# A two-layer sequence model with a third mixer block on one core: each feed-forward part as one program, and matmuls of constants into an unused bank where TensorE waits

## What is computed

```python
# blocks 0 and 1 (i = 0: SSD scan and mLSTM side by side; i = 1: gated linear attention)
h = rmsnorm(x, norm_g[i, 0]);  y = mixer_i(h)            # ends in a product with w_out
x = x + rmsnorm(y, norm_g[i, 1])
h = rmsnorm(x, norm_g[i, 2])
u = dwconv3(h @ ffn_w_up[i]) + conv_b                    # 1024 -> 2 x 2816, 3 taps over tokens
gate, val = split(u)
x = x + rmsnorm((gelu(gate) * val) @ ffn_w_down[i], norm_g[i, 3])
# block 2: causal attention with an index branch, a gated long convolution (31 taps) with a layer norm,
# attention over a memory, three sigmoid gates that merge them, an output projection, 32 routed experts
```

## Time and profile before

| | us |
|---|---|
| median of 3 runs | 2812.07 (2811.98 to 2815.3) |
| profiled execution, its own time | 2814.07 |
| its span | 2812.2 |
| TensorE busy (matmul records) | 2481.3 |
| VectorE, ScalarE, GpSimd busy | 1490.0, 1030.3, 234.3 |
| mean granted TensorE clock | 0.939 |

### The profile page before, as it was taken

The page is one execution under the profiler, slowest core; times in us unless marked ns, Lnnn a source line. Parts: engine busy times, 40 slices in busy tenths (PEclk is TensorE's granted clock), DMA queues, the critical chain, the costliest instruction groups (busy, mean ns, idle before and its releaser), DMA issues. The chain is left out here.

```text
span 2812.2 us, 33931 instructions
## 1 busy us (share of the span) xinstructions
PE 2481.3 (88%) x12483; PEld 2031.4 (72%) x12483; DVE 1490.0 (53%) x2238; ACT 1030.3 (37%) x1718; POOL 234.3 (8%) x264
## 2 busy tenths in 40 slices
PE   5999996688999897998899989799697888599995
PEld 4777785576888785766688877587486677599994
DVE  4766445544555434744555544367897574433333
ACT  3423332334454335423445433433323533133332
POOL 0000001100000000000000000455141000010111
PEclk9999998889999998999999999899897999699997
DMA  4122232122332421112233322223021021699995
GB/s 140 68 83 90 90 105 75 48 88 60 95 100 82 155 80 61 62 59 75 75 97 97 119 105 75 77 89 111 30 74 47 24 90 46 231 373 368 373 377 208
DMA packets 212860, 330.59 MB, mean 118 GB/s; under 512 B 13861, under 2 KB 109997, under 8 KB 212749
## 3 DMA queue, kind: packets, MB, share of 16 engines
q1 hardware_dynamic: 208013, 312.33, 32.4%
q0 software_dynamic: 4736, 16.78, 2.0%
HBM read 299.99 MB, written 29.10 MB: 117 GB/s over the span
## 5 line engine op out<-in xcount | busy, mean ns | idle before, releaser
L366 PE MATMUL ps<-ffn_h_hi,ffn_w_hi 128*128 128x512 f32 x704 | 275.6, 391 | 10.5 <-DVE ffn_h_lo L361 10.5
L367 PE MATMUL ps<-ffn_h_lo,ffn_w_hi 128*128 128x512 f32 x704 | 275.3, 391 | 0.0
L368 PE MATMUL ps<-ffn_h_hi,ffn_w_lo 128*128 128x512 f32 x704 | 275.0, 391 | 0.0
L366 PE MATMUL ps<-wo_hi,lhs_hi 128*128 128x512 f32 x608 | 242.4, 399 | 34.0 <-DVE lhs_lo L361 34.0
L3912 PEld LDWEIGHTS ps<-expert_x,ring 128*128 128x128 f32 x2048 | 235.8, 193 | 8.1 <-DVE expert_x L3995 3.4
L367 PE MATMUL ps<-wo_lo,lhs_hi 128*128 128x512 f32 x608 | 240.8, 396 | 0.0
L368 PE MATMUL ps<-wo_hi,lhs_lo 128*128 128x512 f32 x608 | 240.7, 396 | 0.0
L3912 PE MATMUL ps<-expert_x,ring 128*128 128x96 f32 x2048 | 235.6, 276 | 3.8 <-DVE expert_x L3995 3.0
L361 POOL TENSOR_TENSOR w_lo<-ring,w_hi 128x512 fp32r<-128x512 f32 (+1 forms) x112 | 160.5, 1434 | 750.9 <-ACT w_hi L518 750.2
L361 DVE TENSOR_TENSOR wo_lo<-ring,wo_hi 128x1024 fp32r<-128x1024 f32 x76 | 93.0, 1223 | 185.5 <-ACT wo_hi L653 185.5
L2245 DVE SCALAR_TENSOR_TENSOR y_tmp<-ps,pcol,y_tmp 128x511 f32<-128x511 f32 x88 | 61.9, 745 | 219.8 <-ACT y_tmp L2217 219.8
(11 more groups left out here) (625 smaller groups left out, 5220.9 us busy)
## 6 DMA issues: line engine op xcount, KB each, us to landing
ring<-in_w_up SPq DMA_DIRECT2D x32, 2048.0 KB, 11.1
ring<-in_ffn_w_up SPq DMA_DIRECT2D x88, 512.0 KB, 4.9
moe_down<-in_w_down SPq DMA_DIRECT2D x32, 1024.0 KB
ring<-in_ab_w_in SPq DMA_DIRECT2D x13, 2048.0 KB, 7.9
ring<-in_w_in SPq DMA_DIRECT2D x11, 2048.0 KB, 7.7
ring<-in_ffn_w_down SPq DMA_DIRECT2D x10, 2048.0 KB, 7.7
ring<-in_c_w_in SPq DMA_DIRECT2D x6, 2048.0 KB, 7.9
expert_results<-expert_y SPq DMA_DIRECT2D x32, 384.0 KB, 7.4
```

The lines of the kernel that those rows point to most:

```text
L366: nc.tensor.matmul(out, left[0], right[0], start=start, stop=False, **more)
L367: nc.tensor.matmul(out, left[0], right[1], start=False, stop=False, **more)
L368: return nc.tensor.matmul(out, left[1], right[0], start=False, stop=stop, **more)
```

## The change

Two things are changed. First, `ffn_up` and the `project_out` behind it become one block, `ffn`. The split operands of both halves share one area (`area`, 16 x 1024 columns), in which the down half's row block n takes the place of up weights and of the split input once these have been multiplied (`down_parts`). The loads of the two gains move to its start, the load of the first down chunk moves ahead by one unit. ScalarE and VectorE split row block 0 (`ROWS_AHEAD`) inside the second but last unit's evacuation, and blocks 1 and 2 inside the last one's. TensorE multiplies row block 0 for token tiles 2 and 3 (banks 4 to 7), then 0, then 1, as their banks come free.

Second, `fill_wait(k, bank, passes)` multiplies the identity with a row of parameters, both F32, into a bank that nothing reads: 128x512, as many times as `passes` says. It stands on TensorE's list at the start of blocks, in the tails of the projections (5, 1 and 1 passes behind `turned(1)`, `(2)`, `(3)`; 1, 0, 1 in the last output projection), and at the end of one `project` call (`fill=6`, behind the wait for a free bank). In the tails a new signal, `turned_read`, holds it back until ScalarE has read bank 0.

The core of the diff:

```diff
+def fill_wait(k, bank, passes):
+    for _ in range(passes):
+        k.nc.tensor.matmul(k.ps[:, bank, :], k.ident[:, :], k.brow[:, 0:BANK], start=True, stop=True)
...
 # norm_to_cm, TensorE:
+            fill_wait(k, NBANKS - 1, 4)
 # project, TensorE, start and end of the block:
+            fill_wait(k, NBANKS - 1, 2)
+            if fill > 0:
+                pe.wait_ge(*k.acc_free(len(accs) - NBANKS + 1))
+                fill_wait(k, len(accs) % NBANKS, fill)
 # project_out, TensorE, start of the block and tail:
+TAIL_FILL, SHORT_FILL = (0, 5, 1, 1), (0, 1, 0, 1)
+            fill_wait(k, NBANKS - 1, 3)
+                if t == 1:
+                    pe.wait_ge(*k.turned_read(1))
+                fill_wait(k, 0, (TAIL_FILL if gain is not None else SHORT_FILL)[t])
 # gated_norm:
+            fill_wait(k, NBANKS - 1, 10)
 # gla_stream:
+            fill_wait(k, 0, 2)
 # conv_norm:
+            fill_wait(k, NBANKS - 1, 8)
 # experts:
+            fill_wait(k, NBANKS - 1, 6)
 # last project of the third block: fill=6
...
 # ffn (new), in place of ffn_up and project_out
+    def down_parts(n):
+        at = [0, 4 * D, 7 * D, 10 * D, 13 * D][n % ROWS_HELD]
+        rows, left = area[:, at:at + 2 * D], area[:, at + 2 * D:at + 3 * D]
+        return [rows[:, 0:D], rows[:, D:2 * D]], [left[:, 0:T], left[:, T:2 * T]]
...
+            sp.dma_start(gnext[:, :], everywhere(next_gain, D)).then_inc(k.param_loaded.sem, 16)
+            sp.dma_start(k.gpost[:, :], everywhere(gain, D)).then_inc(k.param_loaded.sem, 16)
...
-            sp.wait_ge(*k.w_lo_ready(2 * FT))
-            for chunk in down:
-                load_weights(k, sp, chunk)
+            for c in range(len(chunks)):
+                sp.wait_ge(*k.w_lo_ready(2 * FT - 2 if c == 0 else 2 * FT + 4 * (c - 1) if c >= 2 else 2 * FT))
+                load_weights(k, sp, chunks[c])
+            for nxt in after:
+                sp.wait_ge(*k.w_lo_ready(3 * FT))
+                if callable(nxt):
+                    nxt(sp)
+                else:
+                    load_weights(k, sp, nxt)
...
+            def tile(n, t):
+                rows, left = down_parts(n)
+                for half in range(2):
+                    last = product(nc, k.ps[:, 2 * t + half, :], [x[:, t * P:(t + 1) * P] for x in left], [x[:, half * BANK:(half + 1) * BANK] for x in rows],
+                                   n == 0, n == FT - 1, skip_group_check=True)
+                return last
+            def turned(t):
+                pe.wait_ge(*k.norm_ready(t + 1))
+                for c in range(KD):
+                    last = nc.tensor.transpose(k.ps[:, 2 * t + c // NT, (c % NT) * P:(c % NT + 1) * P], scratch[:, t, c * P:(c + 1) * P], k.ident[:, :])
+                last.then_inc(k.acc_ready.sem, 1)
+            fill_wait(k, NBANKS - 1, 4)
+            for n in range(ROWS_AHEAD):
+                pe.wait_ge(*k.w_lo_ready(2 * FT + n + 1))
+                pe.wait_ge(*k.h_lo_ready(KD + n + 1))
+                for t in (2, 3):
+                    tile(n, t)
+                if n == 0:
+                    pe.wait_ge(*k.va(FT - 1))
+                tile(n, 0)
+            pe.wait_ge(*k.va(FT))
+            for n in range(ROWS_AHEAD):
+                tile(n, 1).then_inc(k.products.sem, 1)
+            for n in range(ROWS_AHEAD, FT):
+                pe.wait_ge(*k.w_lo_ready(2 * FT + n + 1))
+                pe.wait_ge(*k.h_lo_ready(KD + n + 1))
+                if n < bulk:
+                    for t in range(NT):
+                        last = tile(n, t)
+                    last.then_inc(k.products.sem, 1)
+            for t in range(NT):
+                if t == NT - 1:
+                    turned(0)
+                for n in range(bulk, FT):
+                    last = tile(n, t)
+                last.then_inc(k.products.sem, 1)
+            for t in range(1, NT):
+                turned(t)
+                if t == 1:
+                    pe.wait_ge(*k.turned_read(1))
+                fill_wait(k, 0, (TAIL_FILL if gain is not None else SHORT_FILL)[t])
...
+                for n in down:
+                    split_down(n)
...
+            def split_down(n):
+                if n % 4 == 0:
+                    act.wait_ge(k.loaded[landed[n // 4][0]].sem, landed[n // 4][1])
+                act.wait_ge(*k.products(FT - 1 if n == 0 else FT if n < ROWS_HELD else FT + n - ROWS_HELD + 1))
+                act.wait_ge(*k.vb(2 + n + 1))
+                rows, left = down_parts(n)
+                nc.scalar.copy(rows[0], down_raw(n)).then_inc(k.w_hi_ready.sem, 1)
+                nc.scalar.copy(left[0], g_cm[:, n, :]).then_inc(k.h_hi_ready.sem, 1)
...
-            for s in range(2):
-                finish(TURNS - 1, s, False)
+            finish(TURNS - 1, 0, False, range(ROWS_AHEAD))
+            finish(TURNS - 1, 1, False, range(ROWS_AHEAD, ROWS_AHEAD + 2))
+            for n in range(ROWS_AHEAD + 2, FT):
+                split_down(n)
+            steps(result, norm, read_out)
...
```

More of the change, by code:

```diff
@@ L372, with project @@
 PER_CM = KD // 2
-def project(k, jobs, src=None, tiles=NT, after=(), cold=False, vector=None, scalar=None, load=None, split=True, depth=PIECES, held=None, fresh=True):
+def project(k, jobs, src=None, tiles=NT, after=(), cold=False, vector=None, scalar=None, load=None, split=True, depth=PIECES, held=None, fresh=True, fill=0):
     nc = k.nc
@@ L2150, in ffn_first, with ffn @@
     return load
-def ffn_up(k, layer, h_hi, h_lo, g_cm, ybuf, w_hi, w_lo, down):
+ROWS_AHEAD = 1
+def ffn(k, layer, gain, next_gain, after):
     nc = k.nc
@@ L2161, in ffn_up @@
     tap2, bias = k.pcol[:, 2 + 2 * layer, 0:2 * FT], k.pcol[:, 2 + 2 * layer, 2 * FT:4 * FT]
+    chunks = out_chunks(k.A["ffn_w_down"][layer], FT)
+    ss, root, ss2, root2 = (k.stat[:, n, 0:NT] for n in range(4))
+    bulk = FT - KEPT
+    scratch = k.ytmp
+    landed = []
+    for _ in chunks:
+        s = sum(k.taken) % 2
+        k.taken[s] += 1
+        landed.append((s, 16 * k.taken[s]))
     def column(cols, i, s, half):
@@ L2168, in bank, with whole @@
         return k.ps[:, 2 * s + half, :]
+    def whole(t):
+        return k.ps[:, 2 * t:2 * t + 2, :].rearrange("p a b -> p (a b)")
     def wait(engine, signal, i, per, more):
@@ L2173, in wait, with up_part, down_raw, steps @@
         engine.wait_ge(sem, i * per + (base + more))
-    with nc.Block(no_gpsimd_drain=True) as block:
+    def up_part(which, s, half):
+        at = (4 * s + 2 * which + half) * KD * P
+        return area[:, at:at + KD * P].rearrange("p (c n) -> p c n", c=KD)
+    def down_raw(n):
+        return k.ring[:, landed[n // 4][0], (n % 4) * D:(n % 4 + 1) * D]
+    def down_parts(n):
+        at = [0, 4 * D, 7 * D, 10 * D, 13 * D][n % ROWS_HELD]
+        rows, left = area[:, at:at + 2 * D], area[:, at + 2 * D:at + 3 * D]
+        return [rows[:, 0:D], rows[:, D:2 * D]], [left[:, 0:T], left[:, T:2 * T]]
+    def steps(lead, middle, trail):
+        for t in range(NT + 2):
+            if t < NT:
+                lead(t)
+            if 1 <= t <= NT:
+                middle(t - 1)
+            if t >= 2:
+                trail(t - 2)
+    def turned_half(t, half):
+        c = slice(half * NT, (half + 1) * NT)
+        return k.h[:, c, t * P:(t + 1) * P], k.ps[:, 2 * t + half, :].rearrange("p (c m) -> p c m", c=NT)
+    with ExitStack() as own:
+        g_cm = k.alloc("ffn_g", [P, FT, T], to=own)
+        area = k.alloc("ffn_parts", [P, 16 * D], F32R, own)
+        gnext = k.alloc("next_gain", [P, D], F32, own)
+        ybuf = k.ytmp[:, 0:2, :].rearrange("p s (h t) -> p s h t", h=2)
+        h_hi, h_lo = (area[:, (8 + 4 * n) * D:(12 + 4 * n) * D].rearrange("p (c t) -> p c t", c=KD) for n in range(2))
+        block = own.enter_context(nc.Block(no_gpsimd_drain=True))
         @block.sync
         def _(sp):
+            sp.dma_start(gnext[:, :], everywhere(next_gain, D)).then_inc(k.param_loaded.sem, 16)
+            sp.dma_start(k.gpost[:, :], everywhere(gain, D)).then_inc(k.param_loaded.sem, 16)
             with sp.Fori(1, TURNS) as i:
@@ L2197, in turn @@
                                 pe.wait_ge(*k.h_lo_ready(c + 1))
-                            last = product(nc, bank(s, half), [part[:, s, half, c, :] for part in (w_hi, w_lo)], [h[:, c, :] for h in (h_hi, h_lo)],
+                            last = product(nc, bank(s, half), [up_part(which, s, half)[:, c, :] for which in range(2)], [h[:, c, :] for h in (h_hi, h_lo)],
                                            c == 0, c == KD - 1)
                     last.then_inc(k.products.sem, 1)
+            def tile(n, t):
[10 more added lines that the diff above has]
+            fill_wait(k, NBANKS - 1, 4)
             turn(0)
@@ L2211, in split, with finish @@
                 for half in range(2):
-                    nc.scalar.copy(w_hi[:, s, half, :, :], up_slot(k, s)[:, :, half, :]).then_inc(k.w_hi_ready.sem, 1)
-            def finish(i, s, ahead):
```

(6 more changed lines are left out.)

77 lines of the change are left out of this document (56 added, 21 removed).

## The result

| | before | after |
|---|---|---|
| median | 2813.69 us (4 runs, 2811.98 to 2815.58) | 2771.65 us (4 runs, 2769.74 to 2772.11) |
| ratio, 95% interval | | 0.9849 (0.9832 to 0.9866) |
| profiled execution, span, granted clock | 2814.07, 2812.2, 0.939 | 2769.74, 2768.0, 0.964 |

A forecast was written before the change was run, and what follows sets the result against it. TensorE sets the time; its waits and the 0.50 clock behind them can be won. 2814.07 - 21.5 (merge) - 19.4 (passes) = 2773.2; the runs' median lies 2.0 lower: 2771 us, range 2756 to 2788.

The forecast's parts named there:

- Part 1: Joint of up and down feed-forward halves, written as one program: 10.8 us saved, twice, 21.5 us.
- (d): Down half's row block 1 comes late because of VectorE's queue: up to 3 us a layer, 2777 us; chance 0.05.
- (f): Merging the feed-forward halves does nothing, since the rows of the first split are late anyway; chance 0.01.
- Part 2: Size of one filler pass on TensorE: two records a call, 0.86 us at full clock; 89 passes, 77 us added.
- Part 3: Passes at the waits, summed site by site: 19.4 us saved, between about 0 and 33.5.
- Output projection of layer 1: Its start, 5.27 us at clock 0.50 behind an `lhs_lo` wait, with three passes ahead: 2.3 us saved.
- Third block: Memory norm 1.5, two starts 3.2, convolution norm and attention 2.1, third `project` 0.2: 7.0 us saved.
- Gated norm and projection 0: Two sites where passes, ten and three, begin with the clock already down: 0.8 us saved at each.
- (a): Passes hold the clock everywhere and none outlasts its wait: 55 us saved, 2757 us; chance 0.14.
- (b): Passes bring nothing on balance, through late sites and clock falls elsewhere: 2790 to 2796 us; chance 0.13.
- (c): Transposes do not hold the clock, so the norm sites bring nothing (-4.4 us): about 2776 us; chance 0.07.
- (e): Passes at clock 0.50 outlast their waits everywhere, 56 us lost less the 21.5: slower, 2847 us; chance 0.04.

The follow-up runs named there:

- passes only: Kernel before plus the changed kernel's passes, feed-forward halves still two programs with no pass between them: 2790.99 us, ratio 0.9927 to the kernel before.
- experiment 1: Changed kernel with every pass taken out, feed-forward parts still one program each: 2787.49 us, ratio 0.9911 to the kernel before.
- experiment 9: Changed kernel with the first down weights asked for 10.9 us later, halves still one program: 2773.97 us, ratio 0.9866 to the kernel before.
- the repeat: Changed kernel run and profiled again with no edit: 2772.36 us, ratio 0.9855 to the kernel before.
- experiment 7: Changed kernel without the ten passes ahead of the gated norm, two of each `project` and six ahead of the experts: 2776.97 us, ratio 0.9874 to the kernel before.
- experiment 8: Changed kernel without the six passes ahead of the experts: 2771.13 us, ratio 0.9856 to the kernel before.
- experiment 6: Changed kernel with every pass replaced by six transposes of the identity into the same bank: 2772.97 us, ratio 0.9859 to the kernel before.
- experiment 5: Changed kernel with ten passes instead of five behind token tile 1's transposes in each of four norm tails: 2782.14 us, ratio 0.9896 to the kernel before.
- experiment 10: Changed kernel with 78 more pass calls at waits it leaves open: 2770.55 us, ratio 0.9850 to the kernel before.

## Why the prediction was right, point by point

**Part 1, 10.8 us a layer.** Measured 10.85 and 10.82 (B to C, E to F); as the difference of the whole, 25.0 us for both layers (21.1 to 28.7), where the forecast was 21.5. The slow clock's share is not fixed: against the two blocks of passes only the merge would be worth 9.6 and 10.6. The 10.8 was met to 0.1 us because the kernel before was profiled once, and the forecast and this difference use the same profile. The idle came out at 0.75 us, not 1.3. The first stop is as foreseen (0.39, forecast 0.4), the second shorter (0.36, not 0.6). Rival (d), row block 1 late by up to 3 us, did not happen; (f) is out by experiments 1 and 9. Experiment 9 also shows that the earlier load, which the prediction counted as part of how the wait goes, was not needed.

**Part 2, the pass.** Two records a call, 178 in all, 0.86 to 0.9 us a call at 1.00 (4.46 for five). Right.

**Part 3, 19.4 us for the passes.** The ratios give (1 - 0.9927) x 2812 = 20.5 us for the passes alone, and (0.9911 - 0.9849) x 2812 = 17.4 on top of the merge. By its terms:

- Tails and feed-forward starts, 2.6 each: measured 2.43 and 2.44 (A to B, D to E). The 0.69 us of idle left is the 0.7 of the prediction.
- Layer 1's start, 2.4: from C to its first product 11.05 us before (1071.53 - 1060.48), 10.35 after (1053.20 - 1042.85), so 0.70 where 0.75 was forecast, and the 5.27 us at 0.50 run at 1.00. What of the latter stays is hidden by the chance in stage C to D.
- Output projection of layer 1, 2.3: from its first product to D 49.54 us before (1363.47 - 1313.93), 47.11 after (1342.81 - 1295.70): 2.4, with a wait of the same 5.0 us ahead. In the repeat it is 48.23, and only 1.3 is won: there the clock fell while the three passes ran (mean 0.66 over 4.15 us), although they began at the same distance behind the last product, 1.98 us.
- Third block: the terms for the memory norm, the two starts, the convolution norm and attention and the third `project` make 1.5 + 3.2 + 2.1 + 0.2 = 7.0. Against the merge alone F to G is 6.2 us shorter after and 8.3 in the repeat. The sum fits, but this stage moves by 2 us with no edit. One term can be read by itself: from the first product of the last output projection to G it is 46.32 us before and 46.34 with the merge alone, 44.70 and 44.74 after, so 1.6 as forecast. How the rest divides was not tested.
- Gated norm and projection 0, 0.8 each: these terms were mis-sized. From the end of the mix's last product to A there are 121.24 us before (670.57 - 549.33) and 121.27 with the merge alone, 120.48 and 120.57 in the two profiles after: 0.7 for both where 1.6 was forecast. Without the gated norm's ten (experiment 7) it is 120.82, so the greater part comes from projection 0's three. Those did what the prediction said of a cold start. They ran at a mean of 0.65 and 0.52 and made the first product 0.6 and 0.3 us later (28.89 us behind the mix before, 29.50 and 29.22 after), but from there to A 92.35 us became 90.98 and 91.35. For the gated norm the premise held in one profile only. The ten passes start 3.28 us behind the last product and ran at 1.00 in the first profile; in the repeat the clock was down for part of them. The timeline after:

```profile
549.01 8.82 PE L295 MATMUL ps<-brow,ident 128*128 128x512 f32 x20 [3.28 <-PEq L1807]
559.43 1.09 PE L2017 MATMUL ps<-ident,q_region 128*128 128x128 f32 x8 [1.60 <-DVE q_region L1973]
561.97 1.97 PE L2017 MATMUL ps<-ident,q_region 128*128 128x128 f32 x8 [1.45 <-DVE q_region L1973]
```

and the same passes in the repeat:

```profile
551.86 10.21 PE L295 MATMUL ps<-brow,ident 128*128 128x512 f32 x20 [3.27 <-PEq L1807]
```

The sets of transposes begin 2.54 us apart, with the merge alone too (564.27, 566.81): VectorE sets their pace, and a set takes 1.97 us even at 0.50. A full clock can shorten only the end: with all sets at 1.09 us, as in the repeat, the last one ended 21.26 us behind the mix instead of 22.39.

- Experts, 0.9: not measurable (experiment 8).

**The rivals.** (a) would have needed every listed restart at full clock: several are not (0.60 and 0.71 in the windows above). (b) falls with experiments 1 and 2. (c) falls with experiment 6. The outlasting of (e) was tried in experiment 5, at full clock: four tails with 3.4 us too much cost 10 to 13 us. The changed kernel does not pay this in the tails, where the passes start at 1.00, as the prediction said. At one place of experiment 10 the mechanism of (e) did occur, passes partly at 0.50 that outlast their block.

**What chance gave.** 4.35 us of the profile's 44.2 lie ahead of A, 1.41 in the repeat, and only the 0.7 of the gated norm and projection 0 is the change's. The forecast gained 41 us, by the median of 2812.07, and 42.0 were measured. It was made from the terms alone; that its middle was hit to 1 us is luck, since the layer 1 stage alone moves by 3.

## What to carry to other kernels

A joint between two programs costs the wait and then the slow clock behind it; writing the two as one list of instructions removed both, and needed neither filler (experiment 1) nor an earlier load (experiment 9). Where a wait must stay, fill it from its start, right behind dense work, and stop short of its end: 2 passes instead of 5 lost 1.2 us a tail, 10 lost 3. Fill only in front of work that TensorE itself bounds, and never in a block that otherwise would end sooner. Do not take the price of a restart from one profile: the same wait was followed by 5.7 us at 0.50 in one execution and by 3.0 in another.

## What the runs showed of the hardware that was not expected

- F32 transposes of 128x128 hold the granted clock at 1.00 through a wait (30 in 3.44 us, then 1.71 us idle), as products do (ten records in 4.46 us, then 0.69 us idle).
- 3.27 us idle behind 1.88 us of passes was followed by 0.52; 1.71 and 0.69 us idle behind 3.4 and 4.5 us of work by 1.00. The length of the idle time alone does not decide: 3.28 us idle behind the mix of layer 0 was followed by 8.82 us at 1.00 in one execution, and in the next by 10.21 us at a mean of 0.86 for the same passes.
- Stages with many short waits vary by 3 us between executions of one kernel (layer 1: 299.96 and 303.10) while the merged feed-forward stage repeats to 0.05 us (349.77, 349.76). With one long wait inside it is 359.33 to 360.62.
- The mean granted clock is a poor measure of what can be won: it rose from 0.964 to 0.979 in experiment 10 with ratios of 0.9849 and 0.9850.
